# The value half of a memory projection with the memory tokens on the partitions

## The reference

```python
def _memory_cross_attention(h, mem_n, wq, wkv, q_g, k_g, wo):
    q = _rms_norm((h @ wq).reshape(B, T, X_HEADS, X_HEAD_DIM), q_g)
    k, v = jnp.split(mem_n @ wkv, 2, axis=-1)
    k = _rms_norm(k.reshape(B, M, X_HEADS, X_HEAD_DIM), k_g)
    v = v.reshape(B, M, X_HEADS, X_HEAD_DIM)
    s = jnp.einsum('bthd,bmhd->bhtm', q, k).astype(jnp.float32) / math.sqrt(X_HEAD_DIM)
    p = jax.nn.softmax(s, axis=-1)
    o = jnp.einsum('bhtm,bmhd->bthd', p.astype(v.dtype), v)
    return o.reshape(B, T, X_HEADS * X_HEAD_DIM) @ wo
```

## Time and profile before

| | us |
|---|---|
| median of 3 runs | 2709.38 (2707.04 to 2709.95) |
| profiled execution, its time | 2714.68 |
| profiled execution, its span | 2712.8 |
| TensorE busy | 2655.0 (98%) |
| weight loads busy | 2131.5 (79%) |
| DVE busy | 1314.7 (48%) |
| ACT busy | 1088.9 (40%) |
| POOL busy | 1233.5 (45%) |
| mean granted TensorE clock | 0.994 of full speed |

### The profile page before, as it was taken

How to read it: one execution, slowest core, us unless ns; L and a number is a source line. 1 busy time by engine, 2 the same in 40 slices (tenths; PEclk the granted TensorE clock), 3 DMA queues, 4 the chain that set the end, 5 groups by cost and what they waited for, 6 DMA issues and landing times.

```text
span 2712.8 us, 36859 instructions
## 1 busy us (share of the span) xinstructions
PE 2655.0 (98%) x13092; PEld 2131.5 (79%) x13092; DVE 1314.7 (48%) x1828; ACT 1088.9 (40%) x1658; POOL 1233.5 (45%) x616
## 2 busy tenths in 40 slices
PE   7999999989999999999999999999899999999999
PEld 6888888866678868888888888887567788788887
DVE  5222259776535545252541213788764354543533
ACT  5322242446644454222342223424575445542222
POOL 4444456762235425444544435578422354344443
PEclk9999999999999999999999999999999999999999
DMA  4334433321234313333333353423112332233332
GB/s 129 99 95 117 116 97 94 74 56 50 59 82 117 101 47 108 97 97 96 91 101 94 100 129 97 107 78 74 51 51 59 98 113 86 63 101 101 93 101 78
DMA packets 487754, 243.90 MB, mean 90 GB/s; under 512 B 49501, under 2 KB 483015, under 8 KB 487623
## 3 DMA queue, kind: packets, MB, share of 16 engines
q1 hardware_dynamic: 487104, 242.02, 32.0%
q10 hardware_dynamic: 518, 0.13, 0.0%
HBM read 239.99 MB, written 2.10 MB: 89 GB/s over the span
## 4 chain that ended last, share of the span: by engine, by line
PE 68%; issue 16%; POOL 8%; DVE 5%; ACT 3%; DVEq 1%; ACTq 0%; POOLq 0%
PE pg L654 20%; PE pg L657 20%; PE pg L660 20%; POOL wL L603 8%; PE pA L748 2%; DVE convb L1767 1%; PE pA L935 1%; PE pA L882 1%; PE pg L680 1%; PE pA L810 1%; PE pg L681 1%; PE pg L682 1%; DVE prob L1933 0%; ACT prob L1178 0%; ACT wH L1178 0%
## 5 line engine op out<-in xcount | busy, mean ns | idle before, releaser
L603 POOL TENSOR_TENSOR wL<-raw,wH 128x1024 fp32r<-128x1024 f32 (+1 forms) x472 | 1090.6, 2312 | 1445.8 <-ACT wH L1178 1442.4
L654 PE MATMUL pg<-gxH,wH 128*128 128x512 f32 (+1 forms) x2384 | 930.2, 390 | 4.7 <-DVE gxL L1626 4.2
L660 PE MATMUL pg<-gxH,wL 128*128 128x512 f32 (+1 forms) x2384 | 923.4, 387 | 0.0
L657 PE MATMUL pg<-gxL,wH 128*128 128x512 f32 (+1 forms) x2384 | 917.6, 385 | 0.0
L1178 ACT ACTIVATE wH<-raw 128x1024 fp32r<-128x1024 f32 (+1 forms) x472 | 476.1, 1009 | 873.2 <-PE pg L660 695.1
L654 PEld LDWEIGHTS pg<-gxH,wH 128*128 128x128 f32 x2384 | 448.4, 188 | 106.9 <-issue 15.9
L660 PEld LDWEIGHTS pg<-gxH,wL 128*128 128x128 f32 x2384 | 448.5, 188 | 90.6 <-issue 3.9
L657 PEld LDWEIGHTS pg<-gxL,wH 128*128 128x128 f32 x2384 | 448.6, 188 | 89.5 <-issue 4.7
L654 PE MATMUL pg<-hH,wH 128*128 128x512 f32 x992 | 392.0, 395 | 4.3 <-POOL wL L603 2.7
L660 PE MATMUL pg<-hH,wL 128*128 128x512 f32 x992 | 394.2, 397 | 0.0
L657 PE MATMUL pg<-hL,wH 128*128 128x512 f32 x992 | 391.4, 395 | 0.0
(11 more groups left out here) (247 smaller groups left out, 2236.3 us busy)
## 6 DMA issues: line engine op xcount, KB each, us to landing
raw<-in_ffn_wi SPq DMA_DIRECT2D x352, 256.0 KB, 3.1
raw<-in_w_in SPq DMA_DIRECT2D x200, 256.0 KB, 3.2
raw<-in_ffn_wo SPq DMA_DIRECT2D x128, 256.0 KB, 3.1
raw<-in_ffn_wo SPq DMA_DIRECT2D x64, 192.0 KB, 2.6
raw<-in_xkv SPq DMA_DIRECT2D x32, 256.0 KB, 3.1
raw<-in_w_out SPq DMA_DIRECT2D x32, 256.0 KB, 3.0
raw<-in_sgu_out SPq DMA_DIRECT2D x32, 128.0 KB, 2.3
raw<-in_conv_out SPq DMA_DIRECT2D x32, 128.0 KB, 2.3
```

Of the source, the lines that this page charges most:

```text
L603: pool.tensor_tensor(wL[:, s % 4, 0:n, :], raw[:, s % 2, 0:n, :], wH[:, s % 4, 0:n, :].bitcast(F32), ALU.subtract)\
L654: mm(o, wH[:, s, k, :], rh(k), start=(k == 0), stop=False)
L657: mm(o, wH[:, s, k, :], rl(k), start=False, stop=False)
L660: last = mm(o, wL[:, s, k, :], rh(k), start=False, stop=(k == kt - 1))
```

## The change

The first four U_XKV units, the keys, stay. The last four are loaded wide and multiplied by by_token, which gets the operands and the number of token blocks as arguments: memH and memL blocks of 128 tokens are stationary, 512 weight columns move. Two banks of 128 tokens by 512 value columns come out, the first signalled by xv_mm, the second by unit_mm. DVE copies them directly to vx, behind the key norm of the first two heads and merged_low 6 and 7, and raises evac by 1 and by 3. The turns, their waits and the copies to tb go. stat 12 stands behind the first of the four value units. SP's program for U_XKV is written out in place of a loop.

```diff
--- before.py
+++ after.py
@@ -334,8 +334,8 @@
         mem_tr = sig("mem_tr", 4)
         mem_h = sig("mem_h", 4)
         mem_l = sig("mem_l", 4)
-        xv_tr = sig("xv_tr", 2)
-        xv_cp = sig("xv_cp", 2)
+        xv_mm = sig("xv_mm", 1)
+        xv_cp = sig("xv_cp", 1)
         x_sq = sig("x_sq", 4)
         xs_mm = sig("xs_mm", 4)
         xst_mm = sig("xst_mm", len(XSTEP))
@@ -529,7 +529,11 @@
                         sp.wait_ge(st_mm, risen(st_mm, l, NSTEP))
                         sp.dma_start(memn, mem[0].rearrange("(a p) d -> p a d", p=P))\
                             .then_inc(memld, 16)
-                for u0, w, n in ((U_XKV, xkv[l], 8), (U_WO, w_out[l], 8), (U_XQ, xq[l], 4)):
+                for h in range(4):
+                    unit(l, U_XKV + h, 0, cols_of(xkv[l], h * P))
+                for i in range(4):
+                    wide(U_XKV + 4 + i, row_tiles(xkv[l], 4 * XDH, i))
+                for u0, w, n in ((U_WO, w_out[l], 8), (U_XQ, xq[l], 4)):
                     with sp.Fori(0, n // 4) as i:
                         for c in range(4):
                             unit(l, u0 + c, i, at_col(w, i * (4 * P) + c * P))
@@ -663,12 +667,12 @@
                     if between:
                         between()
 
-            def by_token(l, u0, done, behind=()):
+            def by_token(l, u0, done, xh, xl, tiles=TT, behind=()):
 
                 for i in range(4):
                     u = u0 + i
                     pe.wait_ge(split_l, risen(split_l, l, u + 1))
-                    for a in range(TT):
+                    for a in range(tiles):
                         if i == 0:
                             pe.wait_ge(evac, risen(evac, l, u0 + a - 3))
                         o = pg[:, (u0 + a) % 4, :]
@@ -677,10 +681,10 @@
                             k = 2 * i + h
                             high = wH[:, u % 4, 4 * h:4 * h + 4, :].rearrange("p a c -> p (a c)")
                             low = wL[:, u % 4, 4 * h:4 * h + 4, :].rearrange("p a c -> p (a c)")
-                            mm(o, gxH[:, k, at], high, start=(k == 0), stop=False)
-                            mm(o, gxL[:, k, at], high, start=False, stop=False)
-                            last = mm(o, gxH[:, k, at], low, start=False, stop=(k == KD - 1))
-                        if a == TT - 1:
+                            mm(o, xh[:, k, at], high, start=(k == 0), stop=False)
+                            mm(o, xl[:, k, at], high, start=False, stop=False)
+                            last = mm(o, xh[:, k, at], low, start=False, stop=(k == KD - 1))
+                        if a == tiles - 1:
                             last.then_inc(unit_mm, 1)
                         elif i == 3:
                             last.then_inc(done, 1)
@@ -828,8 +832,8 @@
                     stat(l, 4, bdon, NCMP)
                     v_rows(1)
 
-                by_token(l, U_SGU, v_mm,
-                         (compressed, key_norm, lambda: stat(l, 5, bdon)))
+                by_token(l, U_SGU, v_mm, gxH, gxL,
+                         behind=(compressed, key_norm, lambda: stat(l, 5, bdon)))
                 for j in range(4, 8):
                     unit(l, U_SGU + j, 0, KD, gH, gL)
                 unit(l, U_Q1, 0, KD, gH, gL)
@@ -1023,23 +1027,12 @@
                 def mem_ready(k):
                     pe.wait_ge(mem_l, risen(mem_l, l, k // 2 + 1))
 
-                def xv_turned(i):
-                    pe.wait_ge(evac, risen(evac, l, U_XKV + 6 + 2 * i))
-                    if i == 1:
-                        pe.wait_ge(xv_cp, risen(xv_cp, l, 1))
-                    for a in range(2):
-                        for hh in range(2):
-                            last = turn(pT[:, (2 * a + hh) * P:(2 * a + hh + 1) * P],
-                                        tb[:, i, hh * M + a * P:hh * M + (a + 1) * P])
-                    last.then_inc(xv_tr, 1)
-
-                for h in range(8):
+                for h in range(4):
                     unit(l, U_XKV + h, 0, KD, lambda k: memH[:, k, :], lambda k: memL[:, k, :], n=M,
                          before=mem_ready if h == 0 else None)
-                    if h == 4:
-                        stat(l, 12, ones)
-                    if h == 6:
-                        xv_turned(0)
+
+                by_token(l, U_XKV + 4, xv_mm, memH, memL, tiles=2,
+                         behind=(lambda: stat(l, 12, ones),))
 
                 def m_ready(k):
                     pe.wait_ge(m_l, risen(m_l, l, k + 1))
@@ -1048,7 +1041,6 @@
                          lambda k: merged_tile(hL, gxL, k), before=m_ready if m == 0 else None)
                     if m == 0:
                         stat(l, 13, ones)
-                        xv_turned(1)
 
 
                 def x_bank(key):
@@ -1056,7 +1048,7 @@
                     if n:
                         pe.wait_ge(xst_out, risen(xst_out, l, n))
                     else:
-                        pe.wait_ge(xv_cp, risen(xv_cp, l, 2))
+                        pe.wait_ge(xv_cp, risen(xv_cp, l, 1))
                     return pT
 
                 def x_norms(h):
@@ -2139,29 +2131,29 @@
                         for a in range(2):
                             last = TS(memn[:, a, :], memn[:, a, :], mst[:, a:a + 1], None, ALU.mult)
                         last.then_inc(mem_sc, 1)
-                for h in range(8):
+                for h in range(4):
                     bank = ready(l, U_XKV + h)
-                    dst = kx[:, h, :] if h < 4 else tb[:, (h - 4) // 2,
-                                                       ((h - 4) % 2) * M:((h - 4) % 2 + 1) * M]
-                    dve.tensor_copy(dst, bank[:, 0:M]).then_inc(evac, 1)
+                    dve.tensor_copy(kx[:, h, :], bank[:, 0:M]).then_inc(evac, 1)
                     if h == 1:
                         squares(kT[:, 0, :])
-                    if h == 5:
-                        normed(l, 12, kT[:, 0, :], g8[:, PAIRS:PAIRS + 1])
-                        dve.drain().then_inc(xk_ok, 1)
-                        squares(kT[:, 1, :])
-                    if 2 <= h < 6:
+                    if h >= 2:
                         merged_low(h + 2)
-                    if h == 6:
-                        dve.wait_ge(xv_tr, risen(xv_tr, l, 1))
-                        dve.tensor_copy(vx[:, :, 0:2, :],
-                                        pT.rearrange("p (a h c) -> p a h c", a=2, h=2))\
-                                            .then_inc(xv_cp, 1)
+                normed(l, 12, kT[:, 0, :], g8[:, PAIRS:PAIRS + 1])
+                dve.drain().then_inc(xk_ok, 1)
+                squares(kT[:, 1, :])
+                for m in range(6, 8):
+                    merged_low(m)
+                for a in range(2):
+                    if a == 0:
+                        dve.wait_ge(xv_mm, risen(xv_mm, l, 1))
+                    else:
+                        dve.wait_ge(unit_mm, risen(unit_mm, l, U_XKV + 8))
+                    src = pg[:, (U_XKV + 4 + a) % 4, :]
+                    last = dve.tensor_copy(vx[:, a, :, :], src.rearrange("p (h c) -> p h c", h=4))
+                    last.then_inc(evac, 1 if a == 0 else 3)
+                dve.drain().then_inc(xv_cp, 1)
                 normed(l, 13, kT[:, 1, :], g8[:, PAIRS:PAIRS + 1])
                 dve.drain().then_inc(xk_ok, 1)
-                dve.wait_ge(xv_tr, risen(xv_tr, l, 2))
-                dve.tensor_copy(vx[:, :, 2:4, :],
-                                pT.rearrange("p (a h c) -> p a h c", a=2, h=2)).then_inc(xv_cp, 1)
 
                 norm(l, 2, lambda k: xnorm_tile(hH, gxH, k), lambda k: xnorm_tile(hL, gxL, k), G_X,
                      residual(l, U_WO, 0.5))
```

## The result

The changed kernel takes 2720.99 us (median of 5 runs, 2720.06 to 2721.89), the kernel before 2709.48 in 5 runs beside it (2707.04 to 2710.75). The ratio is 1.0039, 95% interval 1.0028 to 1.0051: slower by 0.4%, 11.5 us by the medians. The execution profiled of each has a span of 2719.1 against 2712.8 us, 6.3 more, with a granted clock of 0.992 against 0.994.

The account below looks back on a forecast made before the run. TensorE, busy 98% of the span, was taken as the bound; 4.3 + 1.7 + 2.6 - 2 x 0.45 = +7.7 us on the median 2709.38 gave 2717.1 us, range 2706 to 2724.

Parts of the forecast that it names:

- The stream and the turning: TensorE's value half: wider matmuls save 0.58 us per layer, the first dropped turn 0.44, together 1.02 before U_WO's first unit.
- The second turn: TensorE behind stat 13: dropping xv_turned(1) saves 0.45 us per layer.
- Layer 0: U_WO's first unit waits for DVE's copy behind normed(12), squares and two merged_lows: starts 4.3 us later.
- the 0.4 gained: Loads ahead of XKV+7's split: 2 KB rows land sooner, so DVE's chain starts 0.4 us earlier.
- The half speed: TensorE behind layer 0's 5.3 us stop: a stretch at half clock adds 1.7 us.
- Layer 1, the term that was mis-sized: U_WO's first unit in layer 1 starts 2.6 us later, the middle of POOL going first and DVE going on.
- the question of the second turn: Layer 1, shared SBUF port: whether POOL or DVE's merged_low(7) goes next; strictly POOL, losing 3.7 instead of 2.6 us.
- paid there already: Layer 1 behind the stop: the half-speed stretch exists before the change, so the clock adds nothing.
- No collision: Rival, chance 0.25: wide loads come 1.5 us earlier at XKV+7, both merged_lows miss POOL; +0.3, 2709.7 us.
- The stream sets the start: Rival, chance 0.08: DVE's copy is ready in time, TensorE's shorter stream decides U_WO's start; 2701.9 us.
- More collisions: Rival, chance 0.15: merged_low(7) waits for POOL in layer 0 too, second half-speed stretch in both layers; +13.5, 2722.9 us.
- What would show it: Signs in the profile: some 5 us idle before U_WO, DVE's V copy named releaser, PEclk about 0.6, value matmuls 0.23 apart.

Follow-up runs that it names:

- e1: Changed kernel with both merged_lows moved ahead of the key norm normed(12): 2711.35 us, 1.0010 of before.
- e8: Changed kernel with the two V copies directly behind normed(12), ahead of squares and the merged_lows: 2708.41 us, 0.9990 of before.
- e2: Changed kernel with ACT instead of DVE copying the two value blocks out of PSUM: 2703.78 us, 0.9977 of before.
- e3: Changed kernel with 20 matmuls without use filling TensorE's stop ahead of U_WO's first unit: 2717.34 us, 1.0025 of before.
- e7: Changed kernel with ACT copying the value blocks and both merged_lows ahead of normed(12): 2702.02 us, 0.9965 of before.
- e9: Kernel before, unchanged, profiled again in a single execution: 2708.12 us.
- e5: Kernel before with 12 matmuls without use ahead of U_WO's first unit, in layer 1 alone: 2711.64 us, ratio 1.000.
- e10: Kernel before, unchanged, one more profile of a single execution: 2711.93 us.

## Why the prediction came out as it did

**Right: direction and mechanism.** +7.7 was forecast. The profiled spans differ by 6.3, the medians by 11.5; the median, 2720.99, lies 3.9 above the 2717.1 forecast, inside the range but above what the forecast's own bounds (+5.8 to +9.6) allow. The wait, the instructions ahead of it and the slow stretch are those described, and the experiments take them away one by one. The two merged_lows are 3.6 and 3.1 us of the stops (e1), squares some 0.8 more (the stops of e8 are 1.2 shorter than those of e1, and 0.4 of that is that XKV+7's split stands earlier there: 16.22 for 16.58 and 15.03 for 15.55), the key norm's chain and the copy the 1.20 and 0.85 that e8 leaves, and e2 has no stop at all; the clock is 3.4 us in both layers together (e3).

By layers the sum did less well than as a whole: it says +5.55 for layer 0 and +2.15 for layer 1, where the profiles have +6.3 and +0.5. That 7.7 comes near their 6.8 is in part two errors that go opposite ways.

**The stream and the turning.** Forecast 0.58 and 0.44 less before WO0. e2 and e7 show it alone: 23.44 to 23.46 against 24.46, 1.0. The second turn: 0.45 forecast, 0.44 measured. The value matmuls start 0.23 apart.

**Layer 0.** 4.3 forecast, 4.79 measured. From the reciprocal to WO0 it is 9.49 us where the sum had 9.81, so the instructions took 0.3 less than it gave them; but their chain starts 0.8 later than granted, since the wide loads didn't gain the 0.4 and XKV+7's split was itself later. The split of XKV+7 began 869.90 less 853.66, 16.24 us behind the first matmul. ACT's row in the changed kernel:

```profile
869.70 1.06 ACT L1170 ACTIVATE wH<-raw 128x1024 fp32r<-128x1024 f32 x1 [3.78 <-DMA raw<-in_xkv]
```

16.67, later by 0.43. Rows of 2 KB in place of 512 B did not make the loads land sooner here: the median from issue to landing, of narrow and wide xkv loads together, went from 3.1 to 3.0 us, the longest from 4.7 to 5.0. In layer 1 the same split came 1.25 earlier (15.68 against 16.93), but that reference is an execution with late loads: against e9's 15.56 it came 0.12 later. So the 0.4 gained was a term that I took from two medians of other stretches and that no run shows. The half speed: 1.7 forecast, 1.98 and 1.56 measured.

**Layer 1, the term that was mis-sized.** 2.6 forecast, 1.10 measured in the profiles. I placed merged_low(7) between two subtractions of POOL that followed each other directly, and weighed which engine would go first. Those two stood together because the loads were late: ACT's splits for them begin 1.55 us apart there (2217.26 and 2218.81). In the changed kernel POOL's subtractions come one by one, 3.6 us apart, and the two merged_lows wait for one and pass together, 3.23 us, as in layer 0. They begin 24.49 behind the first matmul, where merged_low(6) began 25.18 behind it before: 0.7 earlier, 0.3 more than the 0.4 granted. The other 1.2 us of the error is the collision. So the question of the second turn, on which I drew on the Trainium skill (SBUF — State Buffer, section Who interferes with whom), did not arise; that a two-input DVE instruction that meets POOL's subtraction stands still until POOL's is done is what these rows show (3.27 and 3.23 for two, 2.40 for squares in e8, where 0.69 is usual for one).

**The step that failed: the reference point.** I took layer 1's stop of 2.9 us and its 1.7 of half speed as a property of the kernel before, and wrote that nothing is added for the clock there because it "is paid there already". It is paid in four profiled executions of five, those whose loads come late; this and the mis-sized term above have the same root, that the one profile read was of such an execution. Where it isn't paid, the change adds to layer 1 28.42 - 24.46 = 4.0, 1.56 and -0.44, that is 5.1 in place of 0.5. The profiled execution was 5.3 above the median, which I reported and did not use: it was a sign that it held something which others don't. Against the mean of the five profiled spans of before, 2710.7, the changed kernel's span is 8.4 us more, not 6.3. Of these 2.1 us layer 1's stop and slow stretch are 0.7 (their mean over the five against the one profile read) and the cross attention, told below, 1.0. The rest of the way to 11.5 is the spread of before's median: it was 2709.48 in the five runs beside the change, and 2710.06, 2712.75 and 2711.58 in later sets (34, 19 and 15 runs), where single runs span 2705.35 to 2716.82. Against those the change costs 8 to 11 us, though it was not run beside them. Exactly how often the stop occurs in executions that are not profiled stays open; e5 speaks against never and doesn't settle the share.

**The rivals.** "No collision" would have needed the wide loads to come 1.5 earlier at XKV+7; they came 0.4 later. e1, which takes the merged_lows out, shows its WO0 (25.5 for 25.4 in the rival's own sum), but at a stop of 2.4 the clock stays up. "The stream sets the start" is what e2 and e7 build, and its time of 2701.9 is about theirs. "More collisions": no, the two merged_lows pass behind one subtraction, and behind stops of over 5 us WO0 loses 1.98 and 1.56, not a second 1.7.

**What would show it.** Of the signs given, the idle 5 us, the two merged_lows ahead of the copy, the slow stretch (0.50 for the 0.6 forecast), the counts and the 0.23 came as described, and no new stop came in the query stage. One failed: the V copy is not named as the releaser, the row says "issue".

## What to carry to other kernels

A bank handed to the next stage is evicted by an engine whose list is in order: when an edit moves the eviction, read what stands ahead of it there, up to the next bank's user, and price the stop together with the slow stretch behind it. The new form of the matmuls was worth 1.5 us a layer as computed, and its whole result hung on one copy: on ACT the same edit gains 0.2 to 0.35% instead of losing 0.4%, and with the copy ahead of squares and the merged_lows it is at or just below before (0.9990). And where the profiled execution is off the median by as much as the effect looked for, profile the kernel before more than once: a wait that one profile shows may not be in the next, and a cost called "paid already" is paid only where the wait is.

## What the runs showed of the hardware

- The stops of TensorE ahead of WO0 and what followed. Of 2.40 and 2.11 us (e1), 1.20 and 0.85 (e8): WO0 at full speed, 5.53 to 5.57. Of 2.54, 2.80, 2.98, 3.28, 3.35, 3.27, 5.20 and 6.03 us: WO0 takes 7.0 to 7.5, once 8.43 (behind the 3.28 of e10), so 1.6 to 3.0 us more. I had expected the slow stretch to stay in e1.
- The same happens elsewhere from execution to execution. From the first x_norms matmul to the last value product, the cross attention takes 48.6 us or 49.9 to 50.3 in the same code, the difference being a stretch at half speed or none: in the five profiles of before seven times of ten the longer one, in the change both times, in e2 and e7 none of four (e3 has 50.0 and 49.0). The granted clock over the whole execution is 0.992 in the change, 0.994 in before, 0.997 in e2, 0.996 in e7. A difference of 0.003 of 2700 us is 8 us: of the 11.8 us between the spans of before and e2 (2712.8 and 2701.0), only 2.9 are matmuls and transposes, 4.6 the stop in layer 1 with its slow stretch and 3.1 the attention, the rest lies in other stretches; why e2 and e7 pass the attention at full speed each time wasn't tried.
- The first float32r matmul behind a statistics matmul, whose operands are plain float32, is followed by the next one 0.64 us later (890.18 to 890.82 in the change), where 0.23 is usual.
